# Attention of block 2: one step per round, one group of dense blocks per round, both heads scaled on VectorE

## The reference, cut to what matters

```
p = softmax(q @ k.T * 64**-0.5 + mask)   # per head and block of 128 queries
y = p @ v
nsa:  gate0 * (compressed, 31 keys) + gate1 * (selected keys) + gate2 * (window)
fox:  mask also adds a running sum of log forget gates
mem:  256 memory keys, no mask
dsa:  mask from the 128 best scores of an indexer
out = y * silu(z)
```

## Time and profile before

| | |
|---|---|
| Median of 3 runs | 3283.98 us (3281.89 to 3284.62) |
| The profiled execution | 3280.6 us |
| Its span in the profile | 3278.4 us |
| TensorE (PE) busy | 3192.9 us, 97% |
| VectorE (DVE) busy | 1925.6 us, 59% |
| ScalarE (ACT) busy | 1418.9 us, 43% |
| DMA | 358.37 MB, 109 GB/s on average |

### The profile page before, as it was taken

One profiled execution on the slowest core, in us unless ns is written; L12 is line 12 of the kernel. 1 busy time (PEld: TensorE's weight loads), 2 busy tenths in 40 slices (PEclk: granted clock), 3 DMA queues, 4 the chain that ended last, 5 costly groups with the idle time before them and its releaser, 6 DMA issues. The chain is left out here.

```text
span 3278.4 us, 51829 instructions
## 1 busy us (share of the span) xinstructions
PE 3192.9 (97%) x20772; PEld 2536.1 (77%) x20772; DVE 1925.6 (59%) x3355; ACT 1418.9 (43%) x2333; POOL 56.8 (2%) x44
## 2 busy tenths in 40 slices
PE   8999999999999999999999999999999999999998
PEld 6777788788877776787888877866778778667786
DVE  6544735677557446446776367644655676546555
ACT  6423523444346225424444234355743443456532
POOL 0010000000000110000000000000000000000000
PEclk9999999999999999999999999999999999999999
DMA  4324432333332324432333245223154343132342
GB/s 166 91 73 136 160 104 89 103 96 92 118 126 87 88 61 172 148 109 84 96 96 109 71 139 156 99 86 82 51 178 131 131 140 123 58 97 65 144 147 68
DMA packets 107693, 358.37 MB, mean 109 GB/s; under 512 B 12680, under 2 KB 13064, under 8 KB 104784
## 3 DMA queue, kind: packets, MB, share of 16 engines
q1 hardware_dynamic: 107472, 355.33, 33.5%
HBM read 310.57 MB, written 38.81 MB: 107 GB/s over the span
## 5 line engine op out<-in xcount | busy, mean ns | idle before, releaser
L225 PE MATMUL banks<-h_high,weights_high 128*128 128x512 f32 x2448 | 979.4, 400 | 21.6 <-DVE weights_low L246 12.5
L227 PE MATMUL banks<-h_high,weights_low 128*128 128x512 f32 x2448 | 955.9, 390 | 0.0
L226 PE MATMUL banks<-h_low,weights_high 128*128 128x512 f32 x2448 | 955.5, 390 | 0.0
L225 PEld LDWEIGHTS banks<-h_high,weights_high 128*128 128x128 f32 x2448 | 460.6, 188 | 134.6 <-DVE weights_low L246 14.2
L227 PEld LDWEIGHTS banks<-h_high,weights_low 128*128 128x128 f32 x2448 | 460.4, 188 | 98.1
L226 PEld LDWEIGHTS banks<-h_low,weights_high 128*128 128x128 f32 x2448 | 461.2, 188 | 92.5 <-issue 2.9
L1863 DVE TENSOR_TENSOR weights_low<-ring,weights_high 128x1024 fp32r<-128x1024 f32 (+2 forms) x124 | 164.6, 1327 | 293.6 <-ACT weights_high L1809 293.3
L1809 ACT CAST weights_high<-ring 128x1024 fp32r<-128x1024 f32 (+2 forms) x124 | 140.6, 1134 | 439.9 <-PE banks L227 439.7
L213 ACT CAST weights_high<-ring 128x1024 fp32r<-128x1024 f32 x131 | 137.3, 1048 | 374.8 <-PE banks L227 369.8
L218 DVE TENSOR_TENSOR weights_low<-ring,weights_high 128x1024 fp32r<-128x1024 f32 x131 | 161.7, 1235 | 193.3 <-ACT weights_high L213 192.1
L2007 ACT CAST weights_high<-ring 128x1024 fp32r<-128x1024 f32 (+1 forms) x116 | 132.5, 1143 | 321.6 <-PE banks L227 321.6
(11 more groups left out here) (471 smaller groups left out, 4883.7 us busy)
## 6 DMA issues: line engine op xcount, KB each, us to landing
ring<-in_in SPq DMA_DIRECT2D x136, 512.0 KB, 4.2
ring<-in_up SPq DMA_DIRECT2D x88, 512.0 KB, 3.5
ring<-in_gates SPq DMA_DIRECT2D x72, 512.0 KB, 4.2
x<-in_gates SPq DMA_DIRECT2D x56, 512.0 KB, 4.3
ring<-in_down SPq DMA_DIRECT2D x32, 704.0 KB, 4.1
ring<-in_out SPq DMA_DIRECT2D x32, 512.0 KB, 3.6
ring<-in_branch SPq DMA_DIRECT2D x16, 768.0 KB, 4.3
stored<-g_spill SPq DMA_DIRECT2D x16, 768.0 KB, 4.6
```

The source lines that it names most:

```text
L225: pe.matmul(bank, core.wh[:, half, w], high, start=start, stop=False)
L226: pe.matmul(bank, core.wh[:, half, w], low, start=False, stop=False)
L227: return pe.matmul(bank, core.wl[:, half, w], high, start=False, stop=stop)
```

## The change

The double rounds go. Each round has one step: T(s), V(s-1), L(s+4), then one group of dense blocks, 4 in rounds 0 to 23 and 2 in the rounds before 0 and from 24 to 47. The sum stays 152. V is a round later than T. VectorE scales both heads, and `ready` counts two for each step; the semaphores `inverted` and `scaled` go. On ScalarE the exponentials are those of step s+3, on VectorE `normalise(s+2)` comes ahead of `output` and `mask(s+4)`. What each instruction computes is unchanged.

```diff
-    around = range(-2, count // 2 + 1)
-    assert count % 2 == 0 and all(s % 2 for s in finished)
+    around = range(-4, count + 1)
...
             def transposes(s):
                 if not has(s):
                     return
-                pe.wait_ge(sems["ready"], s + 1)
-                pe.wait_ge(sems["scaled"], s + 1)
+                pe.wait_ge(sems["ready"], 2 * s + 2)
...
-            for d in around:
-                transposes(2 * d)
-                extra_products(pe, sems, core, e, ("between", d))
-                transposes(2 * d + 1)
-                extra_products(pe, sems, core, e, ("turned", d))
-                values(2 * d)
-                values(2 * d + 1)
-                logits(2 * d + 4)
-                logits(2 * d + 5)
-                extra_products(pe, sems, core, e, ("last", d))
+            for s in around:
+                transposes(s)
+                values(s - 1)
+                logits(s + 4)
+                extra_products(pe, sems, core, e, ("step", s))
...
-            def scale(s):
-                if not has(s):
-                    return
-                act.wait_ge(sems["inverted"], s + 1)
-                l = probs[s % 4][:, 1, 0:width(s)]
-                act.mul(l, l, stats[:, s % 4, 5:6]).then_inc(sems["scaled"], 1)
-
...
-            for d in around:
-                extra_evacuations(act, sems, core, e, ("last", d - 1))
-                evacuate(2 * d)
-                exps(2 * d + 2)
-                evacuate(2 * d + 1)
-                exps(2 * d + 3)
-                extra_highs(act, sems, core, e, ("last", d - 1))
-                scale(2 * d + 2)
-                scale(2 * d + 3)
-            extra_evacuations(act, sems, core, e, ("last", around[-1]))
+            for s in around:
+                extra_evacuations(act, sems, core, e, ("step", s - 1))
+                evacuate(s)
+                exps(s + 3)
+                extra_highs(act, sems, core, e, ("step", s - 1))
+            extra_evacuations(act, sems, core, e, ("step", around[-1]))
...
-                own.tell(sems["inverted"])
-                l = probs[s % 4][:, 0, 0:width(s)]
-                dve.tensor_scalar(l, l, stats[:, s % 4, 4:5], None, ALU.mult).then_inc(sems["ready"], 1)
+                own.settle()
+                for h in range(2):
+                    l = probs[s % 4][:, h, 0:width(s)]
+                    dve.tensor_scalar(l, l, stats[:, s % 4, 4 + h:5 + h], None, ALU.mult).then_inc(sems["ready"], 1)
...
-            for d in around:
-                output(2 * d - 1)
-                mask(2 * d + 2)
-                mask(2 * d + 3)
-                if d == -1:
+            for s in around:
+                normalise(s + 2)
+                output(s - 1)
+                mask(s + 4)
+                if s == -3:
                     extra_low(dve, sems, core, e, 1)
-                normalise(2 * d + 2)
-                normalise(2 * d + 3)
-                extra_lows(dve, sems, core, e, ("last", d - 1))
+                extra_lows(dve, sems, core, e, ("step", s - 1))
...
-BESIDE_LATER = (2, 6, 4, 4, 4, 4, 4, 4, 6, 2, 6, 2)
...
-    for d in range(-2, steps // 2 + 1):
-        n = BESIDE_LATER[d - 12] if 12 <= d < steps // 2 else 0
-        between, turned, last = (0, 0, 4) if d < 0 else (2, 3, 3) if d < 12 else (n // 2, n - n // 2, 0)
-        slots += [(("between", d), between), (("turned", d), turned), (("last", d), last)]
+    for s in range(-4, steps + 1):
+        slots.append((("step", s), 4 if 0 <= s < steps // 2 else 2 if s < steps else 0))
```

More of the change, by code:

```diff
@@ L3018, in half @@
         return slice(64 * h, 64 * h + 64)
-    with phase(nc, *EXTRA, "forgotten", "logit_mm", "masked", "exped", "inverted", "ready", "scaled", "t_mm", "t_out", "pv_mm",
+    with phase(nc, *EXTRA, "forgotten", "logit_mm", "masked", "exped", "ready", "t_mm", "t_out", "pv_mm",
                "y_out", "own", landed=core.landed[1]) as (block, sems):
```

## The result

The changed kernel took 3293.84 us, median of 7 runs (3290.31 to 3294.24), the kernel before 3283.98 us (3281.89 to 3284.98, 7 runs) on the same chip. The ratio is 1.0029, with a 95% interval of 1.002 to 1.0039: 9.9 us slower. The forecast was 3290.4 us in a range of 3281 to 3299, with half of the chance on slower. The direction and the range held; 3.4 us of the size were missing.

A forecast was written before the change was run, and what follows sets the result against it. The prediction took TensorE's queue, busy for 97% of the span, as the bound. Its terms summed to +3.2 us per layer, +6.4 us in all, from 3283.98 to 3290.4 us, range 3281 to 3299.

The forecast's parts named there:

- 6, opening: Opening of each attention phase: single logits steps between pairs of dense blocks add borders, +0.8 us per layer.
- 8 and 9, scaling, V late: VectorE scaling both heads, and value products a round later, were both costed at nothing.
- Terms 3 and 7: Value products on TensorE: one group per step, +2.4 us per layer; second-last step's products before the last dense block, +0.8.
- Step 4: Logits on TensorE: one group per step, 22 more groups at 0.07 us, +1.5 us per layer.
- Step 1: TensorE's wait for ScalarE's copy between dense tiles goes at 13 borders, 0.1 returning at step 0: -6.9 us per layer.
- Step 2: Transposes now followed by value products cost +8.4 us per layer; in 11 rounds no longer following logits, -0.7.
- Steps 5 and 7: Dense blocks regrouped, -3.1 us per layer; value products ahead of the last dense block, no longer under the final store, +0.8.
- VectorE sets the pace: Rival, chance 0.17: VectorE limits eight wide masked steps, each round 0.5 us longer, 4 us a layer, 3298 us.
- Borders are waits: Rival, chance 0.08: TensorE's border costs are semaphore waits that can go; all gives 3253 us, half 3272.
- No border cost from T to V: Rival, chance 0.14: transposes followed by value products pay no border on TensorE, 4.6 us less per layer, 3281 us.
- The bank wait stays: Rival, chance 0.06: ScalarE comes late to the dense tile's copy, behind the exponentials; +6.9 us a layer, 3304 us.

The follow-up runs named there:

- p_pairs: Kernel before's double rounds, with values a round late, values and logits in pairs, two dense groups, VectorE scaling both heads: 3269.02 us, ratio 0.9957 to before.
- a_pair_both: Changed kernel, but values and logits of two steps are issued together in every second round: 3267.27 us, ratio 0.9953 to the kernel before.
- p_ahead: p_pairs with VectorE taking the masks a pair of steps earlier, behind the normalisation: 3268.64 us, ratio 0.9954 to the kernel before.

## Why the prediction was right or wrong, point by point

The mechanism was right: TensorE's queue sets the time, the bank wait goes, and more borders between kinds of work eat it and more. One term was much too small; the forecast change was 6.4 us and the measured one 9.9. Per layer, in us, the forecast against what the starts of the groups show:

| term | forecast | measured |
|---|---|---|
| 1, bank wait | -6.9 | -7.0 |
| 2, T to V, and T no longer behind L | +7.7 | +7.6 |
| 3, V one group per step | +2.4 | +2.3 |
| 4, L one group per step | +1.5 | **+4.15** |
| 5, D | -3.1 | -3.3 |
| 6, opening | +0.8 | +0.9 and +2.2; shortest against shortest +0.8 |
| 7, V(46) before the last dense block | +0.8 | +0.8 |
| 8 and 9, scaling, V late | 0 | 0 |

Terms 3 and 7 both hold the head of V(46), so the forecast has 0.15 us a layer twice.

**Step 4 failed.** I compared a 384-wide step with other logits behind it, 0.75 us, with one that has dense blocks behind it, 0.82, and took the 0.07 between them as all that a group costs. But both rows belong to pairs. The first holds the entry into L, with no exit; the second the exit, with no entry, and stands behind a step of 31 columns, where 384 columns come out only 0.03 us cheaper than alone. A lone group has both ends: 0.85 us for 384 columns, and 0.34 for 31. In the earlier trace rows the same two steps stand together and take 0.75 + 0.23 = 0.98 us; alone they are 1.19, so a split costs 0.21. The other order, 31 columns first, costs 0.12 to split (1.07 against 1.19). I had asked of V what a head costs, and of L only what a tail costs. Of the 22 pairs in the parts 19 cost about 0.20 and three, with 31 columns first, 0.11 to 0.12: 4.15 us a layer. That is 2.65 above the term, 5.3 in all; the other terms of the parts gave back 0.5 a layer. So 6.4 + 5.3 - 1.1 = 10.6 us, against 9.9 between the medians. Logits in pairs took this term out again (3.94 us a layer of the parts, 10.0 us between the medians).

**Step 1** held even at step 0: T(0) and L(4) alone are 0.31 + 0.63 = 0.94 us, just past the 0.93 of the copy, so the 0.1 that I left for it did not come back. That the wait itself was time, and not a label on time that would have been spent anyway, is shown by the moved border (T 6.4 us a layer shorter, 10.6 us between the medians, of which 1.4 are the even layout).

**Step 2** came from one pair of rows in another phase and was exact: 0.31, 0.53 and 0.75 us, and 0.96 for eight transposes, for 47 of 47 borders. By the same "Mode switching requires drain" of the Trainium skill ("TensorEngine Tiling (Array Packing)", section "Key Properties") the logits, on 64 rows, are a mode too, so both their borders should pay. The trace agrees that both borders cost, with 0.20 us a group; had I held the rule against L as I did against V, I would have looked for a lone group's price.

**Steps 5 and 7:** four blocks behind L take 2.86 us and two 1.50, as assumed. The end of the phase is the DMA as before, 4.72 to 4.74 us from the last dense matmul in both kernels, and SyncE's wait is the same as in the earlier trace rows; so V(46) ahead of that matmul is paid in full.

**The rivals.** *VectorE sets the pace* (0.17) would have given nearly the same total as was measured, 3298 against 3294, and would have passed for the cause without the runs. It is refuted: one head back on ScalarE gains nothing, and twice the scaling costs nothing. I had put VectorE at about 57 us in the second part; it has 50.83. *Borders are waits* (0.08) falls: TensorE shows no wait for another engine in the parts, and each lone group still pays; it stops paying where two groups of its kind touch. *No border cost from T to V* (0.14) falls by the 0.31 us, and by the run with dense blocks in between. *The bank wait stays* (0.06) falls by the 4.2 us on the page, 3.8 of them put down to another cause in the openings.

p_pairs, with the same grouping of V and L as a_pair_both, lies 1.35 us a layer above it, all in the second part. Start by start the two have the same groups, and the excess sits where waits are marked: four L groups are 0.26 to 0.29 us longer, and one D in front of a T 0.16. So about half of the 2.6 us of waits is paid. In p_ahead one L (0.53 us), one D (0.17) and one T (0.35) are longer instead.

What stays open: how often the openings take their long form, and with it 1 to 2 us of the total; why a logits step behind one of 31 columns saves only 0.03 us; and what the array does at a border. The runs give the price of one, not its cause.

## What to carry to other kernels

Where TensorE's queue is the time, count groups and not only instructions: price a group from a row where it stands alone, between the neighbours that it will have, since a row out of a pair lacks its entry or its exit. A wait for a copy out of an accumulating bank can be filled with small groups that exist already: moving the tile border in the kernel before gave 10.6 us (1.4 of them by evener groups), splitting every pair for the same purpose lost 9.9, and the same order with V and L kept in pairs gave 15.9. Before blaming the engine that got the additional work, double that work once; here it was free.

## What the hardware showed that I had not expected

A group of four fp32 logits on 64 rows of the array costs some 0.20 us beyond its columns from 128 columns on: alone, 0.34 us for 31 columns, 0.42 for 128, 0.63 for 256, 0.85 for 384 and 1.06 for 512, so 0.21 for each 128 columns and 0.21 on top, while two steps of 256 in one group take 1.06. About half lies at the entry (31 columns take 0.23 us without it, 0.34 alone) and half at the exit (384 columns take 0.75 us without it, 0.85 alone).

In an opening TensorE runs for a time at the lower level of its clock (1.2 GHz, 0.43 us from one 512-column matmul to the next, against 0.23 later), after idle times of 1.6 to 1.9 us before its first logits and 1.9 us before its first dense matmul, and how long differs with the same code. Of the four openings of the changed kernel shown above, three took 8.72 to 8.95 us at a granted clock of 0.81 to 0.83, and one 10.10 us at 0.70. A single profile can so move by more than 1 us with no edit at all, which is why the parts, equal within 0.01 us in both layers, are the better ruler.
